# Decay factors of a chunked scan: written back to the PSUM bank of their exponents, or to a buffer in SBUF

## The reference, cut to what matters

```
acum = cumsum(dA_c, axis=1)
seg = acum[:, :, None] - acum[:, None, :]
decay = exp(where(causal, seg, -inf))
cb = einsum('blgn,bsgn->blsg', C_c, B_c)
y_diag = einsum('blsg,blsgr,bsgrp->blgrp', cb, decay, xdt_c)
y_off = einsum('blgn,bgrpn,blgr->blgrp', C_c, state, exp(acum))
new_state = state * exp(acum[:, -1]) + einsum('bsgn,bsgr,bsgrp->bgrpn', B_c, to_end, xdt_c)
```

## Time and profile before

| What | Value |
|---|---|
| median of three runs | 1881.79 us |
| the profiled execution: span from its first to its last instruction | 1879.9 us |
| what the median lies above that span | 1.9 us |
| TensorE (PE), busy | 1780.4 us (95%) |
| TensorE's weight loads (PEld), busy | 1236.6 us (66%) |
| VectorE (DVE), busy | 913.8 us (49%) |
| ScalarE (ACT), busy | 718.1 us (38%) |
| GpSimd (POOL), busy | 695.7 us (37%) |

### The profile page before, as it was taken

How to read it: one execution, slowest core, us unless ns; L and a number is a source line. 1 busy time by engine, 2 the same in 40 slices (tenths; PEclk the granted TensorE clock), 3 DMA queues, 4 the chain that set the end, 5 groups by cost and what they waited for, 6 DMA issues and landing times. The chain is left out here.

```text
span 1879.9 us, 29242 instructions
## 1 busy us (share of the span) xinstructions
PE 1780.4 (95%) x9708; PEld 1236.6 (66%) x9708; DVE 913.8 (49%) x2041; ACT 718.1 (38%) x1854; POOL 695.7 (37%) x799
## 2 busy tenths in 40 slices
PE   6999999999998899999999999999998999999994
PEld 3444444687454688888887546468546888888882
DVE  5687754687123454334334622057344634434347
ACT  0443200465023554544444401044235454444541
POOL 1333300165122685554543410300144955554540
PEclk9999999999999899999999999999998999999997
DMA  9865567731105799999996603100237999999964
GB/s 335 308 233 191 191 206 244 255 134 37 64 23 194 258 333 352 330 330 323 330 325 145 219 30 135 57 1 1 73 138 273 321 331 332 318 335 347 335 161 165
DMA packets 170255, 409.50 MB, mean 218 GB/s; under 512 B 37652, under 2 KB 45188, under 8 KB 170164
## 3 DMA queue, kind: packets, MB, share of 16 engines
q1 hardware_dynamic: 132724, 337.77, 50.0%
q0 software_dynamic: 37440, 70.56, 15.1%
HBM read 394.23 MB, written 79.75 MB: 252 GB/s over the span
## 5 line engine op out<-in xcount | busy, mean ns | idle before, releaser
L1336 ACT ACTIVATE arena<-psum,lncol 128x128 f32<-128x128 f32 x1024 | 371.5, 468 | 416.1 <-PE psum L834 416.1
L856 PE MATMUL psum<-arena 128*128 128x128 f32 x4096 | 501.1, 278 | 0.0
L856 PEld LDWEIGHTS psum<-arena 128*128 128x128 f32 x4096 | 478.4, 193 | 1.0 <-issue 1.0
L1871 DVE COPY arena<-arena 128x1 f32 (+1 forms) x128 | 19.7, 154 | 463.8 <-PE psum L856 321.6
L868 PE MATMUL psum<-arena 128*128 128x512 f32 x512 | 241.0, 593 | 0.7 <-DVE arena L1889 0.7
L2250 POOL DMA_INDIRECT expert_sum<-arena,idx x124 | 199.0, 1605 | 39.9 <-issue 38.7
L1889 DVE SCALAR_TENSOR_TENSOR arena<-psum,arena 128x512 f32<-128x512 f32 x256 | 182.0, 744 | 15.0 <-PE psum L868 14.8
L834 PEld LDWEIGHTS psum<-ident,arena 128*128 128x128 f32 x1024 | 122.0, 143 | 74.3 <-issue 64.3
L2221 POOL TENSOR_TENSOR passed<-ones 128x1 f32<-128x1 f32 x252 | 50.4, 200 | 302.3 <-DVE arena L1889 290.8
L2237 POOL DMA_INDIRECT arena<-h_rows,idx x128 | 139.7, 1091 | 19.2 <-issue 4.2
L616 PE MATMUL psum<-arena 128*128 128x512 f32 x320 | 145.5, 616 | 0.0
(11 more groups left out here) (285 smaller groups left out, 2320.6 us busy)
## 6 DMA issues: line engine op xcount, KB each, us to landing
arena<-in_moe_w_dram SPq DMA_DIRECT2D x384, 512.0 KB
arena<-in_ada_w_dram SPq DMA_DIRECT2D x38, 1024.0 KB, 5.2
arena<-in_ssm_w_in_dram SPq DMA_DIRECT2D x9, 2048.0 KB, 11.3
arena<-in_ada_w_dram SPq DMA_DIRECT2D x5, 2048.0 KB, 10.1
arena<-in_ssm_w_out_dram SPq DMA_DIRECT2D x4, 2048.0 KB, 9.1
expert_sum<-arena SPq DMA_DIRECT2D x4, 2048.0 KB, 15.5
arena<-expert_sum SPq DMA_DIRECT2D x16, 512.0 KB, 6.1
arena<-in_kv_ada_w_dram SPq DMA_DIRECT2D x4, 1024.0 KB, 5.9
```

Of the source, the lines that this page charges most:

```text
L856: mm = pe.matmul(psum[:, b, 0:P], w[:, k, :], xeT[u % 2][:, k, :], start=(k == 0), stop=(k == KC - 1))
L1336: ins = act.activation(xeT[u % 2][:, k, :], psum[:, b, P * j:P * j + P], ACT.Identity, scale=h_scale(l, k), bias=h_shift(l, k))
```

## The change

ScalarE's exponential writes its result over its own input, in the PSUM bank of the exponents, and VectorE's multiply reads the factors there. The buffer `decay` and ScalarE's wait before writing it go. The bank is now announced as read (`drained[1 + half]`) by the multiply and no longer by the exponential, and `decay_ready`, which was there unused, tells VectorE that the factors are written. `mixm_ready` goes: TensorE's yd waits for the same multiply by `drained[1 + half]`.

```diff
-        decay = [view(124 + 2 * i, 4 * P) for i in range(2)]
-        mixm_ready = sem("mixm_ready")
@@ TensorE, scan_b
-                        pe.wait_ge(mixm_ready, 2 * q + h // 4 + 1)
+                        until_drained(pe, ("seg", q, h // 4))
@@ ScalarE, scan_exps
                     ps = until_filled(act, ("seg", q, half))
                     if q + 1 < NQ:
                         segments(q + 1, half)
-                    if q:
-                        act.wait_ge(mixm_ready, 2 * (q - 1) + half + 1)
-                    act.activation(decay[half], ps, ACT.Exp).then_inc(drained[1 + half], 1)
+                    act.activation(ps, ps, ACT.Exp).then_inc(decay_ready, 1)
@@ VectorE, scan_g
-                    until_drained(dve, ("seg", q, half))
+                    dve.wait_ge(decay_ready, 2 * q + half + 1)
                     if q:
                         until_filled(dve, ("yd", q - 1))
                     dve.tensor_tensor(mixm[half].rearrange("p (h l) -> p h l", h=4),
-                                      decay[half].rearrange("p (h l) -> p h l", h=4),
-                                      CBm[q % 2].unsqueeze(1).to_broadcast([P, 4, P]), ALU.mult).then_inc(mixm_ready, 1)
+                                      psum[:, 1 + half, :].rearrange("p (h l) -> p h l", h=4),
+                                      CBm[q % 2].unsqueeze(1).to_broadcast([P, 4, P]), ALU.mult).then_inc(drained[1 + half], 1)
```

## The result

The changed kernel takes 1892.18 us (median of 4 runs, 1890.89 to 1896.68), the kernel before, on the same chip, 1882.73 us (4 runs, 1881.12 to 1885.85). The ratio is 1.0055, with a 95% interval from 1.0040 to 1.0071. The profiled span went from 1879.9 to 1889.1 us, +9.2. Forecast were +7.8 and 1889.6 us.

What follows compares the result with a forecast made beforehand. TensorE was taken to bound the scan, VectorE being nearly full; 0.65 + 6.64 + 0.48 + 0.81 - 0.76 = +7.8 us on 1881.79 gave 1889.6 us, range 1883.5 to 1894.5 (the forecast's own 1886.5 to 1893).

Steps and rivals of the forecast that it cites:

- The multiply: VectorE's factor multiply in the scan: 0.68 us each after the change, bounds 0.60 to 1.18; 13 us of busy time back.
- The new wait: TensorE's next exponents wait for VectorE's multiply to free their bank, closing a ring; 0.83 us an ordinary step.
- step 0: First scan step, where ScalarE holds up everyone: exponents' load at 362.65 instead of 362.00, 0.65 us later.
- the release: Time TensorE takes to move after the multiply's end: 0.06 us, bounds 0.05 to 0.12 over 14 waits.
- the giving back: A stalled start on TensorE regains 0.05 us as weights and matmul start together; bounds 0 to 0.1 a stall.
- ordinary: Scan steps q = 1, 2, 4, 6, 8, 10, 12, 14: exponents' load later by 0.83 us each, 6.64 in all.
- before a new chunk: Scan steps q = 3, 7, 11, TensorE doing the sums first: load 0.16 us later each net, 0.48 in all.
- after a turning: Scan steps q = 5, 9, 13, after a turning of y: load 0.27 us later each net, 0.81 in all.
- step 15: Last scan step, without next exponents: quicker multiplies let yd's second half load 2.25 us after yg instead of 3.01, -0.76.
- rival 1: VectorE paces the scan and the change frees it: 13.0 us less, 1868.8 us; chance 0.08.
- rival 2: Multiply's contention with GpSimd stays: second half of the exponents waits too, +17.4 us, 1899; chance 0.06.
- rival 3: The delay is taken up later, at a stage waiting for a transfer that doesn't move: no change, 1882; chance 0.08.

Runs made afterwards that it cites:

- wait-alone kernel: Against the kernel before: factors stay in the SBUF buffer, only the release of the exponents' bank moves from exponential to multiply; 1901.71 us, ratio 1.0104.

## Why the prediction was right, and where it was off

**The bound.** Confirmed. VectorE's 11.9 us brought nothing but the shortened last step.

**The multiply.** Forecast 0.68 us each, measured 0.680. The 32 multiplies lost 13.0 us as forecast (33.5 to 20.5). The contention is gone at every step, as the Trainium skill, "SBUF — State Buffer", section on who interferes with whom, has it for a VectorE instruction with one SBUF input; the wait-alone kernel, with two SBUF inputs, still shows 2.36 us for the pair. Of the 65 ns more for a PSUM source, which the prediction estimated from the Trainium skill, "VectorE: DVE Perf Modes", section on the TRN2 errata, the rows show nothing: 680 ns from PSUM, 684 from SBUF where nothing contends.

**ScalarE.** No difference forecast, 576 against 577 ns measured.

**The new wait.** Its place was as forecast. Of the list of waits the prediction said 9 to 12 us in 14 to 16 pieces: the load's entry fits (10.9 in 16, of which 1.8 us, in step 0, were there before), the matmul's, which names the multiply, doesn't (7.8 in 10). The terms that were mis-sized are the release and the giving back. The prediction took 0.06 us from the multiply's end to the load and gave 0.05 back for a stalled start. The rows show 0.80 from the multiply's start, less its 0.68 that is 0.12, the upper bound of the prediction. And nothing is given back, the lower bound there: from the exponents' first load to the next instruction's it is 1.78 us after a stall (370.21 to 371.99 above), 1.79 before without one. By kind of step:

| Steps | forecast, us | measured, us |
|---|---|---|
| ordinary, 8 | 0.83 each, 6.64 | 0.94 each, 7.52 |
| before a new chunk, 3 | 0.16 each, 0.48 | 0.27 each, 0.81 |
| after a turning, 3 | 0.27 each, 0.81 | 0.38 each, 1.14 |
| step 0 | 0.65 | 0.71 |
| step 15 | -0.76 | -0.71 |
| sum | 7.8 | 9.5 |

Measured values are distances from multiply to load in the rows above against those of the earlier trace rows; for step 15, from yg(14) to the end of yd(15), 456.86 to 460.98 before (4.12 us) and 469.23 to 472.64 after (3.41). The sum agrees with the scan's +9.40. The 1.7 us missing in the forecast are 14 x 0.11 (1.5), 0.06 in step 0 and 0.05 in step 15.

The 0.06 had been rounded up from the 0.05 of the earlier trace rows, which belongs to another load. The exponents' load itself stood idle in the kernel before too, in step 0, and its release was already the longer one:

```profile
361.30 0.58 ACT L1266 ACTIVATE arena<-psum 128x512 f32<-128x512 f32 x1
...
417.31 2.16 DVE L1640 TENSOR_SCALAR arena<-psum,cols 128x128 f32<-128x128 f32 x8 [0.63 <-PE psum L700]
...
419.53 0.14 PEld L660 LDWEIGHTS psum<-ident,arena 128*128 128x128 f32 x1 [0.61 <-DVE arena L1640]
```

The exponential ends at 361.88, the exponents' load starts at 362.00: 0.12. The load of L660, like the one of the earlier trace rows, starts 0.06 after what it waited for (417.31 + 2.16 = 419.47). What sets them apart is the number of events: an exponents' load needs two, its operands (`stepm_ready`) and its bank, the other two loads need one. In the changed kernel's q = 1 the trace has an instruction of TensorE's sequencer, at the line of `claim`, between the multiply's end (369.41 + 0.68 = 370.09) and the load (370.21); it waits for the bank and takes 51 ns:

```profile
L463 PEldq EVENT_SEMAPHORE  x1: 51/51/51, 370.1 to 370.1; - x1
```

Ahead of the loads that need one event there is none. So the 0.12 stood in the trace of the kernel before, at the line that the change was going to stall.

**The rivals.** VectorE as the pace (rival 1) is refuted by the sign. The contention that stays (rival 2) is refuted by the 680 ns; the wait-alone kernel shows that it would have cost about +19. A delay taken up later (rival 3) is refuted by the times of many executions, which follow the scan: by the ratios +10.4 us (7.5 to 13.4) for the changed kernel with a scan of +9.4, and +19.6 (16.0 to 23.0) for wait alone with +18.7. The two profiled spans, +9.2, agree, but by themselves decide little, since parts outside the scan differ by over 2 us from one to the other.

**What stays open.** That the second event makes the release 0.12 us instead of 0.05 is read from the traces; no run changed the number of events. It isn't the contended pair that stood in the earlier trace rows: in the wait-alone kernel such a pair ends at 371.75 and the exponents' load starts at 371.86. The spread of a kernel's runs, 5 us and more, is larger than what tells +7.8 from +9.4; the sizes above rest on traces of one execution each.

## What to carry to other kernels

An edit that reads a value from where it was made, instead of copying it out, also moves the release of that place to the last reader: list who claims the place next, what stands before that claim in its queue, and whether the reader waits, directly or through its queue, for the same engine. If that closes a ring, every instruction in it is paid in each step, at its slot plus the release, and an engine freed by 12 us off the path pays back only what it held up (here 0.7 us, in the last step). Another buffer in the ring, or other work of the waiting engine put ahead of its claim, opens it; but a second wait for the same event in the same queue keeps it shut. The price of a release is to be read at the instruction that will wait for it, not at another one of the same engine.

## What was not expected of the hardware

- From the start of VectorE's 128x512 multiply to the exponents' weight load that waits for it, the rows show 0.80 us each time, with the factors in PSUM or in SBUF: 0.12 after the multiply's shown end. Loads that need only one event start 0.05 to 0.06 after it (and 419.53 above).
- A copy of 128x128 in SBUF shows 0.22 us on VectorE, and the next instruction starts 0.13 after it did; the durations of neighbours overlap.
- An exponential of 128x512 from PSUM takes 576 ns written back to PSUM and 577 to SBUF.
